# A two-layer hybrid encoder on one core: the z projection of two head groups in products of 512 columns over four weight slots, and the middle taps of most convolutions on ScalarE

## The reference

```python
proj = x @ w_in[i]
glu_in, gates, z, xbc, dt_raw = jnp.split(proj, cuts, axis=-1)
# branch A
u = a * jax.nn.sigmoid(gt)                  # GLU of glu_in
u = depthwise_conv_centred(u, conv_w, conv_b)          # 31 taps
# branch B, 8 groups of 4 heads
xbc = jax.nn.silu(depthwise_conv_centred(xbc, conv_w, conv_b))   # 5 taps
y = y_f + y_b + xs * d_skip[:, None]        # chunked scans in both directions
y = y.reshape(b, s, D_INNER) * jax.nn.silu(z)
yg = yg * lax.rsqrt(jnp.mean(jnp.square(yg), axis=-1, keepdims=True) + RMS_EPS)
```

## Time and profile before

| | |
|---|---|
| median of 3 runs | 2442.34 us (2437.61 to 2445.15) |
| the profiled execution, its own time | 2438.85 us |
| span in its profile | 2437.2 us |
| PE busy | 2380.4 us, 98% of the span |
| DVE busy | 1486.2 us, 61% |
| ACT busy | 1370.6 us, 56% |
| POOL busy | 585.9 us, 24% |
| PE's share of the chain that ended last | 84% |

### The profile page before, as it was taken

How to read it: one execution, slowest core, us unless ns; L and a number is a source line. 1 busy time by engine, 2 the same in 40 slices (tenths; PEclk the granted TensorE clock), 3 DMA queues, 4 the chain that set the end, 5 groups by cost and what they waited for, 6 DMA issues and landing times.

```text
span 2437.2 us, 35277 instructions
## 1 busy us (share of the span) xinstructions
PE 2380.4 (98%) x11464; PEld 1944.8 (80%) x11464; DVE 1486.2 (61%) x2553; ACT 1370.6 (56%) x2238; POOL 585.9 (24%) x721
## 2 busy tenths in 40 slices
PE   8999999999999999999999999999999999999998
PEld 6878788887777888887778787888878778888876
DVE  5899999989546111113659989989895451111136
ACT  6755666475564644345567466665746555444455
POOL 3423333242111111111134243332411111111110
PEclk9999999999999999999999999999999999999999
DMA  8576574756787788899664756747577868888884
GB/s 214 125 171 141 132 184 112 162 139 155 173 185 186 165 194 193 188 197 201 160 160 107 183 122 157 164 115 174 119 175 171 204 150 192 191 193 189 196 206 121
DMA packets 111172, 406.04 MB, mean 167 GB/s; under 512 B 12336, under 2 KB 12336, under 8 KB 110768
## 3 DMA queue, kind: packets, MB, share of 16 engines
q0 software_dynamic: 54144, 197.16, 47.4%
q1 hardware_dynamic: 55728, 202.66, 24.2%
q10 hardware_dynamic: 1152, 4.37, 0.5%
HBM read 402.04 MB, written 2.10 MB: 166 GB/s over the span
## 4 chain that ended last, share of the span: by engine, by line
PE 84%; ACT 4%; DVE 4%; DMA 3%; issue 3%; POOL 0%; ACTq 0%; SPq 0%; POOLq 0%; DVEq 0%; another core or an unknown queue 0%
PE bank L835 22%; PE bank L837 22%; PE bank L836 22%; PE bank L878 3%; PE bank L877 3%; PE bank L880 2%; DMA w_raw<-w_stream 2%; PE bank L951 2%; PE bank L957 1%; DMA w_lo<-w_stream 1%; ACT w_lo L465 1%; PE bank L939 1%; ACT w_hi L464 1%; PE bank L1156 1%; PE bank L922 1%
## 5 line engine op out<-in xcount | busy, mean ns | idle before, releaser
L352 POOL DMA_DIRECT2D w_lo<-w_stream x376 | 327.5, 871 | 1576.4 <-ACT w_lo L465 1525.4
L835 PE MATMUL bank<-x_hi,w_hi 128*128 128x512 f32 x1728 | 685.9, 397 | 4.6 <-DMA w_lo<-w_stream 4.6
L837 PE MATMUL bank<-x_hi,w_lo 128*128 128x512 f32 x1728 | 673.8, 390 | 0.0
L836 PE MATMUL bank<-x_lo,w_hi 128*128 128x512 f32 x1728 | 672.8, 389 | 0.0
L464 ACT ACTIVATE w_hi<-w_raw 128x1024 fp32r<-128x1024 f32 x378 | 402.7, 1065 | 287.2 <-PE bank L837 232.0
L465 ACT ACTIVATE w_lo<-w_raw 128x1024 fp32r<-128x1024 f32 x378 | 399.9, 1058 | 0.0
L835 PEld LDWEIGHTS bank<-x_hi,w_hi 128*128 128x128 f32 x1728 | 324.5, 188 | 74.7 <-issue 8.8
L837 PEld LDWEIGHTS bank<-x_hi,w_lo 128*128 128x128 f32 x1728 | 324.3, 188 | 69.0
L836 PEld LDWEIGHTS bank<-x_lo,w_hi 128*128 128x128 f32 x1728 | 324.6, 188 | 68.3 <-issue 3.3
L1238 DVE SCALAR_TENSOR_TENSOR z_a<-glu_out,params,z_a 128x497 f32<-128x497 f32 (+14 forms) x480 | 320.1, 737 | 0.0
L1685 DVE TENSOR_TENSOR glu_out<-bank,sigmoids 128x512 f32<-128x512 f32 x44 | 30.4, 692 | 416.5 <-PE bank L837 416.5
(11 more groups left out here) (242 smaller groups left out, 3611.2 us busy)
## 6 DMA issues: line engine op xcount, KB each, us to landing
w_raw<-w_stream SPq DMA_DIRECT2D x378, 512.0 KB, 4.5
w_lo<-w_stream POOLq DMA_DIRECT2D x376, 512.0 KB, 7.2
z_b<-x_in SPq DMA_DIRECT2D x4, 512.0 KB, 6.9
w_ple_in<-w_ple ACTq DMA_DIRECT2D x2, 1024.0 KB, 11.4
out<-z_b SPq DMA_DIRECT2D x4, 512.0 KB, 7.1
ple_p<-p_in ACTq DMA_DIRECT2D x2, 512.0 KB, 6.7
params<-par_in ACTq DMA_DIRECT2D x2, 340.0 KB, 3.8
tmp_m<-w_dt ACTq DMA_DIRECT2D x2, 256.0 KB, 5.2
```

The costliest lines, as they stand in the source:

```text
L352: gp.dma_start(wlo[:, s, :], w_stream[cyc, s].bitcast(F32R), accum_op=ALU.add).then_inc(lo_done[s], 16)
L835: pe.matmul(dst, wh, mh, start=first, stop=False)
L836: pe.matmul(dst, wh, ml, start=False, stop=False)
L837: return pe.matmul(dst, wl, mh, start=False, stop=last)
```

## The change

The order on PE, ACT, DVE and POOL within `pair` is new, and so is the order of the tiles in the stream.

- z: the 512 columns of z of both groups are packed so that one tile holds two row blocks of 512 columns. `z_pass(c0, n)` multiplies row blocks 2n and 2n+1 into banks 0 to 3, one bank per token chunk; four passes fill the banks. 96 products of 512 columns a pair take the place of 192 of 256. `z_gate` takes silu per chunk, of both groups at once.
- Three of G1's tiles (both xs, B) come before z, and C after it.
- The last pass stands directly before `dense(c0+2, 3)`, whose bank 3 also held the last chunk of z.
- Middle taps: for G0's four tiles, G1's xs tiles and the GLU's two tiles (8 of 10 a pair) ACT writes the middle tap (`middle_tap`, `middle_tap_a`), and `taps` skips it. G1's B and C stay with DVE.
- `square` writes what it squares over z_tok.
- In POOL's order the loads of slot 2 and slot 3 stand elsewhere among the masks.

```diff
+            def middle_tap(g, c, of_):
+                act.activation(feat[:, c, :], of_, ACT.Identity, scale=group_par(g, c * TAPS + TAPS // 2),
+                               bias=group_par(g, 4 * TAPS + c)).then_inc(mid_done, 1)
...
+            def z_gate(pair_, c0, c):
...
+                if c < CH - 1:
+                    act.wait_ge(z_done, seen((CH - 1) * pair_ + c + 1))
+                else:
+                    act.wait_ge(used[2], seen(c0[1] + 3))
+                act.activation(ztok[:, c, :, :].rearrange("p q e -> p (q e)"), bank[c][:, :], ACT.Silu).then_inc(evac[c], 1)
...
+            def z_pass(c0, n, chunks=range(CH), last=True):
+                cyc, s = on(c0, 1 if n == 0 else 2), (n - 1) % SLOTS
+                pe.wait_ge(lo_done[s], 16 * (cyc[0] + 1))
+                for i, c in enumerate(chunks):
+                    if n == 0:
+                        pe.wait_ge(evac[c], seen(c0[1] + (1 if c == CH - 1 else 2)))
+                    t = slice(c * P, (c + 1) * P)
+                    for k in (2 * n, 2 * n + 1):
+                        w = slice(k % 2 * T, (k % 2 + 1) * T)
+                        pe.matmul(bank[c][:, :], xh[:, k, t], whi[:, s, w], start=k == 0, stop=False)
+                        pe.matmul(bank[c][:, :], xh[:, k, t], wlo[:, s, w], start=False, stop=False)
+                        q = pe.matmul(bank[c][:, :], xl[:, k, t], whi[:, s, w], start=False, stop=k == KT - 1)
...
-                z_tiles(on(c0, 1), 0)
-                dense(on(c0, 1), 2, xh, xl)
+                for n in range(3):
+                    dense(on(c0, 1), n, xh, xl)
                 xs_transpose(G0)
                 exponent(G0, 0, True)
-                dense(on(c0, 1), 3, xh, xl)
+                z_pass(c0, 0, (3, 0, 1, 2))
                 b_transpose(G0)
                 c_dot_b(G0)
                 exponent(G0, 1, True)
-                dense(on(c0, 2), 0, xh, xl)
+                z_pass(c0, 1, (0, 1), False)
+                state(G0, 0)
                 exponent(G0, 2)
-                state(G0, 0)
-                dense(on(c0, 2), 1, xh, xl)
+                z_pass(c0, 1, (2, 3))
                 exponent(G0, 3)
                 state(G0, 1)
                 state(G0, 2)
-                z_tiles(on(c0, 2), 2, (0, 1))
+                z_pass(c0, 2)
+                z_pass(c0, 3, (0, 1), False)
                 y_chunk(G0, 0)
-                z_tiles(on(c0, 2), 2, (2,))
+                z_pass(c0, 3, (2,), False)
                 y_chunk(G0, 1)
                 y_chunk(G0, 2)
-                z_tiles(on(c0, 2), 2, (3,))
+                z_pass(c0, 3, (3,))
+                dense(on(c0, 2), 3, xh, xl, ks=low)
                 y_chunk(G0, 3)
+                dense(on(c0, 2), 3, xh, xl, ks=high)
...
-                    conv(g0, G0, 0, [(c0, 0), (c0, 1)])
-                    conv(g0, G0, 2, [(c0, 2), (c0, 3)])
+                    conv(g0, G0, 0, [(c0, 0), (c0, 1)], m0 + 2)
+                    conv(g0, G0, 2, [(c0, 2), (c0, 3)], m0 + 4)
                     weighted_xs(g0, G0, 0)
                     weighted_xs(g0, G0, 1)
+                    conv(g1, G1, 0, [(c0 + 1, 0), (c0 + 1, 1)], m0 + 6)
                     mask_cb(G0)
-                    conv(g1, G1, 0, [(c0 + 1, 2), (c0 + 1, 3)])
```

More of the change, by code:

```diff
@@ L97 @@
 Y_BANKS = (6, 4)
+MIDS = 8
 def on(cyc, n):
@@ L154, in build @@
             btok = sb("b_tok", [P, CH, STATE], F32, r)
-            ztok = sb("z_tok", [P, 2, T], F32, r)
+            ztok = sb("z_tok", [P, CH, 2, GW], F32, r)
             E = sb("decay", [P, CH, HG, P], F32, r)
@@ L637, in pair @@
                 for c in range(CH):
-                    square(G0, c)
-                z_gates(G1, on(c0, 2), (2, 3))
+                    z_gate(L * PAIRS + j, c0, c)
+                square(0, G0, 0)
+                square(0, G0, 1)
+                hi(on(c0, 3), 2)
+                square(0, G0, 2)
+                square(0, G0, 3)
+                take(on(c0, 2), 3, cin[:, 3, :])
+                hi(on(c0, 3), 3)
                 xs_tokens(G1, 0)
@@ L865, in projection @@
                     i.then_inc(used[b], 1)
-            def z_tiles(cyc, s, chunks=range(CH)):
-                if chunks[0] == 0:
-                    slot_ready(cyc, s)
-                    slot_ready(cyc, s + 1)
-                for c in chunks:
-                    dst = halves(bank[s + c // 2])[:, c % 2, :].rearrange("p (b e) -> p b e", b=2)
-                    for k in range(KT):
-                        t, w = slice(c * P, (c + 1) * P), slice(k * P, (k + 1) * P)
-                        h, l, end = whi[:, s:s + 2, w], wlo[:, s:s + 2, w], k == KT - 1
-                        pe.matmul(dst, xh[:, k, t], h, start=k == 0, stop=False)
-                        pe.matmul(dst, xh[:, k, t], l, start=False, stop=False)
-                        if c < CH - 1 or not end:
-                            pe.matmul(dst, xl[:, k, t], h, start=False, stop=end)
-                        else:
-                            pe.matmul(dst[:, 0], xl[:, k, t], h[:, 0], start=False, stop=False).then_inc(used[s], 1)
-                            pe.matmul(dst[:, 1], xl[:, k, t], h[:, 1], start=False, stop=end).then_inc(used[s + 1], 1)
+            def z_pass(c0, n, chunks=range(CH), last=True):
[10 more added lines that the diff above has]
+                        q = pe.matmul(bank[c][:, :], xl[:, k, t], whi[:, s, w], start=False, stop=k == KT - 1)
+                    if last and i == len(chunks) - 1:
+                        q.then_inc(used[s], 1)
+                    elif n == SLOTS - 1:
+                        q.then_inc(z_done, 1)
             def xs_transpose(G):
@@ L1225, in heads, with taps @@
                 return t.rearrange("p (h e) -> p h e", h=HG)
-            def taps(outs, ins, ws, count, finish, between=lambda n: None):
+            def taps(outs, ins, ws, count, finish, between=lambda n: None, mid_made=False):
                 mid = count // 2
@@ L1233, in taps @@
                         a, b = max(0, -o), T - max(0, o)
+                        if n == 0 and mid_made:
+                            continue
                         if n == 0:
@@ L1236, in taps @@
                             continue
-                        dve.wait_ge(dve_order, issued(0 if n == count - 1 and i else 1))
+                        if n > 1 or not mid_made:
+                            dve.wait_ge(dve_order, issued(0 if n == count - 1 and i else 1))
                         q = dve.scalar_tensor_tensor(out=outs[i][:, a:b], in0=ins[i][:, a + o:b + o], scalar=w[:, k:k + 1],
@@ L1244, in taps, with conv @@
                     between(n)
-            def conv(g, G, i, tiles):
+            def conv(g, G, i, tiles, mids=None):
                 for cyc, s in tiles:
@@ L1254, in conv @@
                     dve.wait_ge(yo_done, seen(CH * G))
+                if mids is not None:
+                    dve.wait_ge(mid_done, seen(mids))
                 taps([feat[:, i, :], feat[:, i + 1, :]], [cin[:, i, :], cin[:, i + 1, :]],
@@ L1762, in layout, with conv_cols @@
         for j in range(PAIRS):
-            for g in (2 * j, 2 * j + 1):
-                stream += [cols(wi, XS0 + g * GW), cols(wi, XS0 + g * GW + P), cols(wi, B0 + g * STATE), cols(wi, C0 + g * STATE)]
-                stream += [cols(wi, Z0 + g * GW), cols(wi, Z0 + g * GW + P)]
+            def conv_cols(g):
+                return [cols(wi, XS0 + g * GW), cols(wi, XS0 + g * GW + P), cols(wi, B0 + g * STATE), cols(wi, C0 + g * STATE)]
+            z = wi[:, Z0 + j * 2 * GW:Z0 + (j + 1) * 2 * GW].reshape(SLOTS, 2, P, T)
+            second = conv_cols(2 * j + 1)
+            stream += conv_cols(2 * j) + second[:3]
+            stream += [np.concatenate([z[n, 0], z[n, 1]], 1) for n in range(SLOTS)] + second[3:]
             for t in (2 * j, 2 * j + 1):
```

95 lines of the change are left out of this document (57 added, 38 removed).

## The result

| | before | after |
|---|---|---|
| median, 9 runs each, same chip | 2436.2 us (2430.44 to 2445.15) | 2453.08 us (2447.5 to 2460.11) |
| ratio after to before | | 1.0065, 95% interval 1.0051 to 1.008 |
| the profiled execution | 2438.85 us | 2450.91 us |
| PE busy | 2380.4 us | 2373.4 us |

The change made the kernel slower, by 0.65% or 17 us. The forecast was 0.2%, within what a measurement cannot tell from no change; 0.65% is outside of that. Runs 9, 10 and 11 were measured while the kernel before itself scattered from 2449 to 2832 us, and one execution of run 9 took 4805 us; for those three only their own other times and their traces are used, not a ratio.

A forecast was written before the change was run, and what follows sets the result against it. TensorE, busy 98% of the span, was taken as the bound. Per pair -1.3 - 0.5 + 0.95 + 1.6 = +0.75, taken as +0.7, or +5.6 us over eight pairs: median 2448 us, 8-in-10 range 2430 to 2458.

The forecast's parts named there:

- the case "slower": Outcome where the whole kernel's time rises by more than the 7.3 us a measurement can tell; chance 0.30.
- slow masks before exponents 2 and 3: Rival: GpSimd needs 4.27 us for both G0 masks under DVE, +1.45 us a pair, 2454 us; chance 0.24.
- z, -1.3 a pair: In z, 96 products of 512 columns replacing 192 of 256 save 1.3 us a pair, bounds 0 and 1.35.
- z gains nothing: Rival in z: a 512-column product costs as much as two of 256; 2458 us, chance 0.04.
- The transposes of xs, -0.5: TensorE's wait for the silu of xs before the transposes goes, 0.5 us a pair saved, bounds 0 and 0.52.
- I cost them at nothing: Moving 8 middle taps a pair from DVE to ScalarE adds nothing; at most 0.6 us each if cover failed.
- The bank of the last z chunk, +0.95: The dense behind z's last product waits for ScalarE's gate to read bank 3: +0.95 us a pair, bounds 0.8 and 1.5.
- The exponents, +1.6: TensorE waits for GpSimd's masks before G0's exponents 2 (0.6) and 3 (1.0): +1.6 us a pair, bounds 0.5 and 2.3.
- The third stretch, unchanged: From y_chunk(G0,3)'s end to y_transpose(1,G1): stays 43 to 44 us, keeping 3.1 us of idle TensorE waiting for DVE.

The follow-up runs named there:

- run 9: run 6 with a two-input scalar_tensor_tensor of one column in place of the one-input tensor_scalar; 2453.58 us.
- run 10: run 6 with the added instruction placed between G0's two convolutions instead of ahead of the first; 2438.92 us.
- run 11: run 3 with the order of run 4; 2423.07 us.
- run 6: Changed kernel plus a one-column, one-input VectorE instruction ahead of G0's first convolution, its tile placed last so no other tile moves; 2442.87 us, ratio 1.0009.
- run 12: run 11 with chunk 3 of z finished ahead of chunk 2; 2417.16 us, ratio 0.9896.
- run 7: Kernel before plus only an unused one-column tile (4 bytes a partition) that moves later tiles by 32 bytes; 2427.68 us, ratio 0.996.
- run 2: Kernel before with only the middle taps of G0's four and the GLU's two tiles moved to ScalarE; 2445.63 us, ratio 1.0016.
- run 4: Changed kernel with G0's exponents 2 and 3 spaced apart again by more z products; 2454.77 us, ratio 1.006.
- run 3: Changed kernel plus a one-column, one-input VectorE instruction ahead of G0's first convolution, its tile moving later tiles by 32 bytes; 2428.38 us, ratio 0.995.
- run 8: run 3 with y_chunk(G0,3) moved ahead of the whole dense(c0+2,3); 2428.38 us, ratio 0.9952.
- run 1: Changed kernel with the middle taps of G0's four tiles back on VectorE; 2440.9 us, ratio 0.9998.
- run 5: Changed kernel plus only the unused one-column tile that moves later tiles by 32 bytes, no added instruction; 2450.02 us, ratio 1.0048.

## Why the prediction was right and wrong

The direction was given as the likelier one of two small ones (+0.2%), and the measured +0.65% falls in the case "slower". The mechanism that was priced for that case, slow masks before exponents 2 and 3, is not what made it so. That 2453 lies inside the range, and 1 us from the 2454 of the slow masks, is luck: 10.3 us of it are a wait that the prediction does not have. With that wait gone (run 6) a pair is 0.5 us longer than before, near the +0.7 that was forecast, though there too by two misses that partly cancel: z gives less than forecast, and the exponents cost 0.75 in place of 1.6.

- **z, -1.3 a pair.** 23 steps from 206.72 to 211.96 give 0.2278 each, near the 0.2268 taken, and TensorE's work did shrink. What reached the pair is less: run 12 against run 7, same placement, is 142.26 against 143.40, of which 0.27 are waits (3.81 and 4.08 in sum), so 0.9. The term was too large by 0.4. The rival "z gains nothing" fell, and with it the gap rule of the Trainium skill ("TensorE: Matmul & The Clock Gate", Back-to-back issue gap), by which the gain is estimated at 0.2 us.
- **The transposes of xs, -0.5.** Right: no wait.
- **The middle taps, "I cost them at nothing".** This is the step that failed. The prediction saw that GpSimd stood beside the middle taps, for it read their 1.68 us for two as "with GpSimd beside them", and asked only what their going means for TensorE, VectorE and ScalarE, not what GpSimd loses. In the changed kernel mask 0 is held 12.3 us in six pairs and exponent 0 waits 1.7 there, 10.3 us in all; run 6, which undoes only this, takes 2.3 us off a pair. The contention rule of the Trainium skill ("SBUF — State Buffer", Who interferes with whom) was applied to masks 2 and 3 and not to mask 0, which the sum never names. Run 2 shows a second cost, waits for late weights at z of 3.8 us in all, which the new order of the changed kernel mostly avoids (its waits for low parts in z are 0.8 us in all).
- **The bank of the last z chunk, +0.95.** Right: 0.86 in all eight pairs and about 0.1 for the restart; run 12 without it gains 1.1.
- **The exponents, +1.6.** Right in the second pair, 0.49 + 1.03 = 1.52; over all eight 18.3 - 10.3 = 8.0 us, 1.0 a pair, inside its bounds 0.5 and 2.3. Where exponent 0 waits less, these are smaller: 0.25 + 0.50 in run 6. Run 4 took them away, 6.5 us in six pairs, and these got 5.7 us shorter, though a `y_chunk` waits 0.7 more in each.
- **The third stretch, unchanged.** Right: 43.58 against 43.87.

The second pair in TensorE's rows, from one `y_transpose(1,G1)` to the next: its idle time rose from 3.87 to 7.44 us (+1.70 at exponent 0, +1.52 at exponents 2 and 3, +0.86 at the gate, -0.36 at the transposes, -0.15 at `y_chunk(G1,3)`), and everything else, z and the restarts behind the waits, fell by 0.42: +3.15. From the first `y_transpose(1,G1)` to the last of each layer six pairs grew by 16.7 us; the stages outside them gave some of it back in the profiled execution, which is 12.1 us longer (TensorE's waits for the weights' low parts fell from 8.9 to 5.4 us in all), while the medians differ by 16.9.

What stays open: why a select passes at a one-column, one-input instruction in each of the 36 pairs in which it was waiting (runs 3, 6, 8, 10, 11 and 12, six each), and failed at four full middle taps in one pair of run 1; 2.5 us of what run 2 lost; and, in part, where run 4 lost again what it gave in the pairs.

## What to carry to other kernels

Before an instruction is moved off an engine, ask who else was using the time in which it ran. A cheap instruction with one SBUF input in a long chain of two-input ones can be the only moment at which GpSimd gets its data; if it must go, leave one of a single column in its place, a little after GpSimd's work is issued. When a product's bank is wanted at once by the next one, finish another bank last. And when an edit adds or drops even a 4-byte tile, look where the big operands now begin.

## What the runs showed that I had not expected

- A GpSimd select of 0.65 us is held 12.3 us by 18 two-input VectorE instructions in a row, and freed by a VectorE instruction of 0.15 us with one input (2.75 us for two selects).
- Products whose moving operand begins 32 bytes off a multiple of 64 in the partition step by 0.2333 us, and by 0.2267 where the same tile begins at a multiple of 64; products on x, which begins at a multiple of 64 in both kernels, take the same time. Other offsets were not tried. An unused tile of 4 bytes makes the kernel before 0.4% faster (run 7).
- The mean granted clock was not the same for all kernels: 0.995 to 0.996 over the runs of the kernel before that stood beside runs 1 to 8 and 12, 0.998 in the changed kernel, 0.997 to 0.998 in runs 1, 3, 4, 6, 8 and 12, but 0.995 in run 2 and 0.994 in runs 5 and 7. Of the runs of the kernel before beside runs 1 to 4, the five at 0.993 or 0.994 took 2446.8 us on average and the ten at 0.996 or 0.997 took 2439.5; beside runs 5 to 8 the difference was 2 us. So some of the few us that the waits do not explain may be the clock's.
- What a slower stretch costs depends on where it falls. In the kernel before, three of them, 3.41 us each at a granted clock of 0.50, lie in the last three pairs, each behind a wait of TensorE of 1.4 us for `tmp_y`. The first of them:

```profile
1491.98:1495.39 3.41, 3.41 (x9) 2.65 (x9) 3.21 (x9) 0.73 (x3) 1.05 (x2) 0.50 0.76 155
```

Those pairs are as long as the others (143.7 us): TensorE's wait of 1.7 us for VectorE before `y_transpose(1,G1)`, which the first five pairs have, is gone in them, and the slower products stand in its place.
